# Token mixers: values stationary, two heads in the column halves, division ahead of the turn

## The reference

```python
p = jax.nn.softmax(sc, axis=-1).astype(v.dtype)          # branches a and c
return jnp.einsum('bhqk,bhkd->bhqd', p, v)
...
w = jnp.where(mask, jnp.exp(jax.nn.log_sigmoid(z) + suffix), 0.0)   # branch b
return jnp.einsum('bhqk,bhkd->bhqd', w, v)
...
g = jax.nn.sigmoid(gates.reshape(bsz, s_len, N_BRANCH, D_MODEL) + b_gate)
ys = jnp.stack([y_a, y_b, y_c], axis=2)
merged = jnp.einsum('bsnk,nkd,bsnd->bsd', ys, w_branch, g)
```

## Time and profile before

| | us |
|---|---|
| median of three runs | 2231.26 |
| the profiled execution | 2227.12 |
| its span, first to last instruction | 2225.3 |
| TensorE busy | 2011.0 (90%) |
| VectorE busy | 1413.3 (64%) |
| ScalarE busy | 850.5 (38%) |

### The profile page before, as it was taken

The page is one execution under the profiler, slowest core; times in us unless marked ns, Lnnn a source line. Parts: engine busy times, 40 slices in busy tenths (PEclk is TensorE's granted clock), DMA queues, the critical chain, the costliest instruction groups (busy, mean ns, idle before and its releaser), DMA issues.

```text
span 2225.3 us, 26662 instructions
## 1 busy us (share of the span) xinstructions
PE 2011.0 (90%) x9732; PEld 1486.1 (67%) x9732; DVE 1413.3 (64%) x2159; ACT 850.5 (38%) x1106; POOL 65.3 (3%) x93
## 2 busy tenths in 40 slices
PE   3999899989999999999988999886899879879987
PEld 2788788867887788778876887665544347654442
DVE  6888777656898888776756898775421147642111
ACT  3334555645434444555555343542200035320000
POOL 0000000000000000000000000110000001000000
PEclk9999999999999999999999999997899989989999
DMA  9898444426897799554425898541799985359997
GB/s 397 353 368 348 180 180 142 143 94 245 332 375 303 279 368 375 197 180 137 154 107 192 321 376 296 186 148 51 282 422 421 421 323 206 96 187 410 421 421 310
DMA packets 98178, 597.91 MB, mean 269 GB/s; under 512 B 20240, under 2 KB 23696, under 8 KB 27408
## 3 DMA queue, kind: packets, MB, share of 16 engines
q1 hardware_dynamic: 91600, 585.18, 67.1%
q10 hardware_dynamic: 6464, 11.15, 1.6%
HBM read 595.21 MB, written 1.09 MB: 268 GB/s over the span
## 4 chain that ended last, share of the span: by engine, by line
PE 64%; DVE 12%; DMA 12%; ACT 5%; issue 4%; POOL 1%; SPq 0%; ACTq 0%; DVEq 0%; POOLq 0%
PE acc L1950 10%; PE acc L1953 9%; PE acc L1954 9%; PE gu L2299 9%; PE gu L1950 6%; PE gu L1954 5%; PE gu L1953 5%; PE tr L2299 5%; DMA w_raw<-wstream 4%; DMA proj<-ada_stream 4%; DVE w_lo L1159 3%; PE tr L2048 3%; PE acc L2299 3%; DMA stage<-wstream 2%; ACT w_hi L654 2%
## 5 line engine op out<-in xcount | busy, mean ns | idle before, releaser
L1159 DVE TENSOR_TENSOR w_lo<-stage,w_hi 128x2048 fp32r<-128x2048 f32 x233 | 532.1, 2287 | 76.9 <-ACT w_hi L654 76.5
L654 ACT ACTIVATE w_hi<-stage 128x2048 fp32r<-128x2048 f32 x233 | 444.5, 1912 | 247.6 <-PE acc L1954 243.6
L1217 DVE SCALAR_TENSOR_TENSOR proj<-proj,c_row 128x1024 f32<-128x1024 f32 x240 | 291.6, 1218 | 52.9 <-DMA proj<-ada_stream 41.9
L1950 PE MATMUL acc<-w_hi,hT_hi 128*128 128x512 f32 (+1 forms) x736 | 307.5, 418 | 18.1 <-DVE hT_lo L1819 12.6
L1950 PE MATMUL gu<-w_hi,hT_hi 128*128 128x512 f32 x704 | 284.7, 404 | 21.3 <-DVE pair L1287 10.5
L1953 PE MATMUL acc<-w_lo,hT_hi 128*128 128x512 f32 (+1 forms) x736 | 292.1, 397 | 0.0
L1954 PE MATMUL acc<-w_hi,hT_lo 128*128 128x512 f32 (+1 forms) x736 | 291.7, 396 | 0.0
L1954 PE MATMUL gu<-w_hi,hT_lo 128*128 128x512 f32 x704 | 278.6, 396 | 0.0
L1953 PE MATMUL gu<-w_lo,hT_hi 128*128 128x512 f32 x704 | 278.2, 395 | 0.0
L1950 PE MATMUL acc<-w_hi,yT_hi 128*128 128x512 f32 (+1 forms) x460 | 183.0, 398 | 8.4 <-DVE yT_lo L1693 5.7
L1953 PE MATMUL acc<-w_lo,yT_hi 128*128 128x512 f32 (+1 forms) x460 | 180.4, 392 | 0.0
(11 more groups left out here) (224 smaller groups left out, 2333.6 us busy)
## 6 DMA issues: line engine op xcount, KB each, us to landing
stage<-wstream SPq DMA_DIRECT2D x332, 1024.0 KB, 6.0
proj<-ada_stream SPq DMA_DIRECT2D x120, 1024.0 KB, 7.8
w_raw<-wstream SPq DMA_DIRECT2D x96, 1024.0 KB, 16.8
tok<-gate_rows SPq DMA_DIRECT2D x10, 512.0 KB, 4.4
tf<-bgate_in ACTq DMA_DIRECT2D x12, 256.0 KB, 4.7
proj<-rel_in ACTq DMA_DIRECT2D x16, 192.0 KB, 2.4
z_mix<-wstream SPq DMA_DIRECT2D x2, 1024.0 KB, 17.4
once<-wstream SPq DMA_DIRECT2D x2, 1024.0 KB, 24.9
```

The source lines that it names most:

```text
L654: act.activation(w_hi[:, n % PARTS, :], stage[:, n % STAGES, :], ACT.Copy).then_inc(hi_ready, 1)
L1159: dve.tensor_tensor(w_lo[:, n % PARTS, :], stage[:, n % STAGES, :], w_hi[:, n % PARTS, :].bitcast(F32), ALU.subtract).then_inc(chunk_ready, 1)
L1217: ins = dve.scalar_tensor_tensor(w, w, 1.0, c_row[:], ALU.mult, ALU.mult, accum_out=dst)
L1950: ins = pe.matmul(dst, l_hi, r_hi, start=start, stop=False, skip_group_check=True)
```

## The change

- **out_pair** takes the place of out, once for two heads in even slots (2, 4, ... 22) and at the end, ahead of the weights' turn or suffix. The values (128 keys x 64) are stationary, the turned weights move (256 columns for the first key tile, 128 for the second); head e of the pair writes rows 64 e to 64 e + 63 of one bank, so the result is the output turned. Pairs 0 to 7 use acc, pairs 8 to 11 tr.
- **divide** on VectorE scales prob by 1 / rsum before TensorE turns it, which waits for it (w_ready). emit becomes one copy of 128 x 256 for a pair.
- **The yT turns** are gone; y_high and y_low read the stored outputs in SBUF (mixed, split), in slots 10, 17, 21 and at the end. TensorE's B fills wait for y_ready.
- **Slots 16 to 23**: suffix waits for argument(s - 2) instead of emit; weigh waits for the last pair that read its buffer.
- **The end**: hi and lo of the last fill's chunk (that of the second B chunk after slot 23) stand behind weigh and argument of slot 23; the sigmoids of branch 1's two gate blocks stand together behind them, with no table load back; y_high and y_low of the last two pairs stand before take_block half 1 of slot 23.

```diff
-      10: [("yT", 2, 0), ("yT", 2, 1)], 11: [("sT", 2)], 12: [("sT", 3)], 17: [("yT", 0, 0), ("yT", 0, 1)]}
+      11: [("sT", 2)], 12: [("sT", 3)]}
+SLOT_SPLITS = {10: [(2, 0), (2, 1)], 17: [(0, 0), (0, 1)], 21: [(1, 0)], SLOT_HEADS: [(1, 1)]}
...
+if slot > 2 * NH and slot % 2 == 0:
+    use("oT", slot // 2 - 1)
...
-    for r in range(2):
-use("yT", 1, r)
+    use("oT", SLOT_HEADS // 2 - 1)
...
-    "mixer": dict(n=MIX_CHUNKS, u=len(MIX_TR), th=8, tf=2, req=1, src=1, sc=24, mx=16, pr=24, ov=24, st=8, mg=4,
+    "mixer": dict(n=MIX_CHUNKS, u=len(MIX_TR), th=8, tf=2, req=1, src=1, sc=24, mx=16, pr=24, ov=8, st=8, mg=4,
...
+w_ready = sem("w_ready")
+y_ready = sem("y_ready")
...
+def mixed(n, r):
+    src = mv if n == 2 else proj[:, :, (1024, 2560)[n]:(1024, 2560)[n] + 512]
+    return src[:, :, 2 * r * P:2 * (r + 1) * P].rearrange("p t (a e) -> p a t e", a=2)
+def split(dst, r):
+    return dst[:, 2 * r:2 * r + 2, :].rearrange("p a (t e) -> p a t e", t=NT)
...
         def weigh(s_):
...
-            act.wait_ge(o_full, b["ov"] + s_ - 1)
+            if s_ < 2 * NH + 2:
+                act.wait_ge(o_full, b["ov"] + NH)
+            else:
+                act.wait_ge(tr_full, b["u"] + MIX_TR["oT", s_ // 2 - 1] + 1)
...
         def y_high(n, r):
-            u = b["u"] + MIX_TR["yT", n, r]
-            act.wait_ge(tr_full, u + 1)
-            d = yT_hi[:, 2 * r:2 * r + 2, :].rearrange("p a s -> p (a s)")
-            act.activation(d, tr[:, u % 2, :], ACT.Copy).then_inc(th_ready, 1)
+            if n == 1:
+                act.wait_ge(tr_free, b["u"] + MIX_TR["oT", 2 * NH // 2 + 2 * r + 1] + 1 + 2)
+                used(MIX_PRE + MIX_FILL.index(("B", 0, 1)))
+            else:
+                act.wait_ge(o_free, b["ov"] + (4 if n == 2 else 8))
+                used(MIX_PRE + MIX_FILL.index(("B", 2, 1)) if n == 0 else 5)
+            act.activation(split(yT_hi, r), mixed(n, r), ACT.Copy).then_inc(th_ready, 1)
...
         def sigmoid(blk):
...
-            act.preload_act_table_set("natural_log_exp_and_others")
+            if n != 1:
+                act.preload_act_table_set("natural_log_exp_and_others")
...
         for s_ in range(SLOT_HEADS):
...
-            hi(n0 + c + 2)
+            if s_ < SLOT_HEADS - 1:
+                hi(n0 + c + 2)
...
-            for what in SLOT_TURNS.get(s_, []):
-                if what[0] == "yT":
-                    y_high(*what[1:])
+            for what in SLOT_SPLITS.get(s_, []):
+                y_high(*what)
...
                 weigh(s_)
-            if s_ and MIX_FILL[s_ - 1][0] == "G" and block_ends(s_ - 1):
+            if 0 < s_ < SLOT_HEADS - 2 and MIX_FILL[s_ - 1][0] == "G" and block_ends(s_ - 1):
...
+        for what in SLOT_SPLITS[SLOT_HEADS]:
+            y_high(*what)
+        hi(n0 + MIX_PRE + SLOT_HEADS + 1)
+        sigmoid(FILL_BLOCK[SLOT_HEADS - 3])
...
-        y_high(1, 0)
-        y_high(1, 1)
...
-        inv_at = {}
...
-        def emit(s_):
-            h, a = s_ % NH, s_ % 2
-            dve.wait_ge(o_full, b["ov"] + s_ + 1)
-            if s_ >= 2 * NH:
-                o = acc[:, a, 0:P].rearrange("p (q e) -> p q e", q=NT)
-                dve.tensor_copy(proj[:, :, 2560 + h * HD:2560 + (h + 1) * HD], o).then_inc(o_free, 1)
-                return
-            dve.wait_ge(dve_up, inv_at[s_])
-            for q in range(NT):
-                dst = mv[:, q, h * HD:(h + 1) * HD] if s_ < NH else proj[:, q, 1024 + h * HD:1024 + (h + 1) * HD]
-                ins = dve.tensor_scalar(dst, acc[:, a, q * P:q * P + HD], rinv[:, a, q:q + 1], None, ALU.mult)
-            ins.then_inc(o_free, 1)
+        def emit(d):
+            n = BRANCHES[d // 4]
+            if d < NH:
+                dve.wait_ge(o_full, b["ov"] + d + 1)
+                o, freed = acc[:, d % 2, 0:S], o_free
+            else:
+                u = b["u"] + MIX_TR["oT", d]
+                dve.wait_ge(tr_full, u + 1)
+                o, freed = tr[:, u % 2, 0:S], tr_free
+            at = P * (d % 4) + (0, 1024, 2560)[d // 4]
+            dst = (mv if n == 2 else proj)[:, :, at:at + P]
+            dve.tensor_copy(dst, o.rearrange("p (t e) -> p t e", t=NT)).then_inc(freed, 1)
...
         def turn_weights(s_):
-            nonlocal ups
...
-            if s_ >= 2:
-                dve.wait_ge(o_free, b["ov"] + s_ - 1)
...
-            ups += 1
-            inv_at[s_] = ups
-            dve.reciprocal(rinv[:, s_ % 2, :], rsum[:, s_ % 2, :]).then_inc(dve_up, 1)
+        def divide(s_):
+            a = s_ % 2
+            dve.wait_ge(p_ready, b["pr"] + s_ + 1)
+            own(dve.reciprocal(rinv[:, a, :], rsum[:, a, :]))
+            for q, (at, end) in enumerate(((0, 128), (128, 384))):
+                ins = dve.tensor_scalar(prob[:, a, at:end], prob[:, a, at:end], rinv[:, a, q:q + 1], None, ALU.mult)
+            ins.then_inc(w_ready, 1)
...
         def y_low(n, r):
-            u, i = b["u"] + MIX_TR["yT", n, r], 2 + 2 * BRANCHES.index(n) + r
+            i = 2 + 2 * BRANCHES.index(n) + r
...
-            dve.tensor_tensor(flat(yT_lo[:, 2 * r:2 * r + 2, :]), tr[:, u % 2, :],
-                              flat(yT_hi[:, 2 * r:2 * r + 2, :]).bitcast(F32), ALU.subtract).then_inc(tr_free, 1)
+            dve.tensor_tensor(split(yT_lo, r), mixed(n, r), split(yT_hi, r).bitcast(F32),
+                              ALU.subtract).then_inc(y_ready, 1)
...
         enter(0)
         for s_ in range(SLOT_HEADS):
...
-            if s_ >= 2:
-                emit(s_ - 2)
             if s_ + 1 < SLOT_HEADS:
...
-            lo(n0 + MIX_PRE + s_ + 2)
+            if s_ == 0:
+                divide(0)
+            if s_ < SLOT_HEADS - 1:
+                lo(n0 + MIX_PRE + s_ + 2)
...
                 argument(s_)
...
                 take_block(s_, 0)
+            for what in SLOT_SPLITS.get(s_, []):
+                y_low(*what)
...
-                if what[0] == "yT":
-                    y_low(*what[1:])
-                else:
-                    at = 2 * what[1] + (8 if what[0] == "sT" else 0)
-                    copy_turn(what, flat(qk[:, at:at + 2, :]))
+                at = 2 * what[1] + (8 if what[0] == "sT" else 0)
+                copy_turn(what, flat(qk[:, at:at + 2, :]))
+            if s_ and s_ % 2 == 0:
+                emit(s_ // 2 - 1)
...
+            if s_ + 1 < 2 * NH:
+                divide(s_ + 1)
...
                 argument(s_)
+            if s_ == SLOT_HEADS - 1:
+                emit(s_ // 2)
+                for what in SLOT_SPLITS[SLOT_HEADS]:
+                    y_low(*what)
...
                 take_block(s_, 1)
-        emit(SLOT_HEADS - 2)
-        emit(SLOT_HEADS - 1)
-        y_low(1, 0)
-        y_low(1, 1)
+        lo(n0 + MIX_PRE + SLOT_HEADS + 1)
...
                 take_block(s_, t)
...
         def turn_weights(s_):
-            pe.wait_ge(p_ready, b["pr"] + s_ + 1)
+            pe.wait_ge(w_ready, 2 * NH * l + s_ + 1)
...
         def suffix(s_):
...
-            pe.wait_ge(o_free, o0 + s_ - 1)
+            if a < 2:
+                pe.wait_ge(o_free, o0 + NH - 1 + a)
+            else:
+                pe.wait_ge(arg_ready, b["st"] + a - 1)
...
-        def out(s_):
-            h, pT = s_ % NH, probT[:, s_ % 2, :]
-            if s_ < 2 * NH:
-                copied("turn", s_)
+        def out_pair(d):
+            if d < NH:
+                copied("turn", 2 * d + 1)
+                o, full = acc[:, d % 2, 0:S], o_full
+                if d >= 2:
+                    pe.wait_ge(o_free, o0 + d - 1)
...
-                pe.wait_ge(p_ready, b["pr"] + s_ + 1)
-            if s_ >= 2:
-                pe.wait_ge(o_free, o0 + s_ - 1)
-            pitch = P if s_ < 2 * NH else HD
-            o = acc[:, s_ % 2, :]
-            def v(kt):
-                if s_ < NH:
-                    return mv[:, kt, h * HD:(h + 1) * HD]
-                at = (1024 if s_ < 2 * NH else 2560) + h * HD
-                return proj[:, kt, at:at + HD]
-            if s_ == NH:
-                pe.wait_ge(fill_out[1], f0 + 2)
-            elif s_ == 2 * NH:
-                pe.wait_ge(fill_out[1], f0 + 5)
-            small_mm(o[:, 0:HD], pT[:, 0:128], v(0))
-            small_mm(o[:, pitch:pitch + HD], pT[:, 128:256], v(0), True, False)
-            small_mm(o[:, pitch:pitch + HD], pT[:, 256:384], v(1), False, True).then_inc(o_full, 1)
+                pe.wait_ge(p_ready, b["pr"] + 2 * d + 2)
+                u = u_of("oT", d)
+                pe.wait_ge(tr_free, u + 1)
+                o, full = tr[:, u % 2, 0:S], tr_full
+            if d % 4 == 0 and d:
+                pe.wait_ge(fill_out[1], f0 + (2 if d < NH else 5))
+            for kt in range(NT):
+                for e in range(2):
+                    at = (0, 1024, 2560)[d // 4] + HD * (2 * (d % 4) + e)
+                    v = (mv if d < NH // 2 else proj)[:, kt, at:at + HD]
+                    pT = probT[:, e, 0:S] if kt == 0 else probT[:, e, S:S + P]
```

(23 more changed lines are left out.)

## The result

The changed kernel takes 2194.18 us in the median of four runs (2187.84 to 2198.06), the kernel before 2230.98 (2227.66 to 2234.28): a ratio of 0.9837, 95% interval 0.9819 to 0.9855. The prediction was 2199, with a range from 2191 to 2214. The profiled execution of the changed kernel took 2198.06 us, 29.1 less than the profiled one of before.

What follows compares the result with a forecast made beforehand. TensorE was taken to bound the slots, three waits the mixers' end. Terms gave 15.0 us in the first mixer and 17.4 in the second, together 32.4, taking the median from 2231.3 to 2199 us; range 2191 to 2214.

Steps and rivals of the forecast that it cites:

- 12 pairs of heads: Per mixer: out_pair replaces two separate products per pair at 0.94 us, gaining 0.31 us a pair, 3.7 us in all.
- slot 0: First slot of each mixer: TensorE's weight transposes wait for divide, costing 0.85 us; bounds 0 to 1.5.
- turns of the outputs: Slots 10 and 17: transposes of the branch outputs go, saving 2.10 and 0.87 us, 2.97 per mixer.
- slot 20: TensorE stalls 1.65 us ahead of its first fill where it stalled 0.3: 1.35 us lost, bounds 0.4 and 2.5.
- stalls that went: Slot 20 and ahead of the last suffix: waits of suffix for emit go, gaining 1.26 us with restarts.
- end, less its pair: Last suffix to last branch's first fill: 15.48 us becomes 7.4; gain 8.1, or 7.7 without the pair already counted.
- clock: Around the mixers' ends: half clock goes with the idle time, regaining 1.6 us in the first mixer, 4.0 in the second.
- the charge for the old products: Per pair of heads: two old products counted as 1.25 us, 1.34 less what the one beside the scores shares.
- The tiling mode: Each pair, two mode changes: priced at 0.15 us each from the experts' matmuls; at 0.39 each the pair loses 0.17.
- The cover of about 4 us: From slot 1 on: divide is queued about 4 us before TensorE wants it, so it is free there.
- the chain: Slots 18 and 19: fill, splits, product, weigh, sigmoid with table loads, next splits and product; about 16.5 us against TensorE's 14.8.
- both covers: At the end: weigh finishes under a 2.8 us fill; last emit, y_high and y_low, about 2.05 us, under the other.

## Why the prediction was right

**The sum and its place.** The sum said 15.0 and 17.4 us for the two mixers; 15.97 and 18.09 came. All of it lies where the sum put it, and the time is 4.8 us below the forecast's: 1.7 of it from the mixers, the other 3.1 is less than what two medians of this kernel differ by for equal code (those of the kernel before beside the runs here went from 2226.84 to 2231.85). The stage lost 6.1 us ahead of the last suffix, 8.1 and 9.6 from there to the branch fill, and 1.8 and 2.4 behind it. The terms, one by one, per mixer, from start to start of TensorE's instructions in the first:

| term | predicted us | measured us | by |
|---|---|---|---|
| 12 pairs of heads | 3.7 | 4.2 | slots 7 and 8 14.92 to 14.53, slots 2 and 3 14.77 to 14.35, slots 17 and 18 15.99 less the turns' 0.87 to 14.81 |
| slot 0 | -0.85 | -0.78 | fill to turn, 3.05 to 3.83 |
| turns of the outputs | 2.97 | 3.0 | slots 9 and 10: 16.62 to 14.09, less the pair; slot 17: 0.87 |
| slot 20 | -1.35 | -1.38 | 24 fill matmuls 7.36 for 5.64, less the 0.33 of before |
| stalls that went | 1.26 | 1.4 | ahead of the suffix of slot 20 and of the last one, against the same instructions in the slots beside them |
| end, less its pair | 7.7 | 7.8 | 15.48 to 7.41 |
| clock | 1.6 and 4.0 | 1.8 and 4.0 | behind the end 14.31 and 14.92 to 12.54; second end 17.05 for 15.48 |

The measured terms add up to 16.0 and 18.2, within 0.2 us of what the stages lost. The terms of turns and stalls are read from the two traces; no experiment takes them out one by one.

**The pair** was the mis-sized term. Its own cost was right (0.94 predicted, 0.95 measured), but what it replaced was worth more: it gains 0.39 to 0.41 us up to slot 15 instead of 0.31. The step that was off is the charge for the old products, 1.25 us for two; 0.95 and 0.39 make it 1.34. The lone product was taken for 0.67 us and is worth 0.72: 0.58 to the next start, and 0.14 because without it 24 fill matmuls follow each other directly and take 5.57 us, where the two fills around it took 2.85 and 2.86. The product beside the scores was taken for 0.58 and is worth 0.62. In slots 16 to 22, where a suffix and not a turn stands behind the pair, it gains only 0.3: the way back costs 0.11 us there instead of 0.06, which is half of the difference.

**The tiling mode.** The eight passes lie between matmuls of full width. Of their 0.95 us the passes themselves are 0.64, as forecast: putting the second head in the same half adds just that (1.45 for 0.80). What is left for going in and coming back is 0.31, half of it inside the 0.80, where 0.15 and 0.15 were taken from the row of the experts' stage. The Trainium skill (TensorEngine Tiling (Array Packing), Key Properties) says that a change of the tiling mode drains TensorE. The trace has a cost of some 0.15 us at each change, which agrees with it and doesn't show a drain by itself; at this price it decided nothing.

**The division** was covered in every slot but the first, and slot 0 was 0.07 us off. The cover of about 4 us, on which this stood, is there from slot 3 on (3.7 to 5.6 us from the scalings' end to the turn); in slot 1 it is 0.68 and in slot 2 2.49. Doubling the scalings still cost nothing in the other slots, but slot 1 is close: it is the one that waits when slot 0 no longer does. VectorE's share rose to 80% and no slot was set by it.

**Slots 18 to 20** went as the chain said: one stall, ended by a block product, 1.71 us for 1.65 with its restart, and it went with the sigmoid out of the chain, which gave 1.68.

**The end** came to the hundredth (7.4 predicted, 7.41 measured), since all its terms were TensorE's own durations once both covers held. Both did: weigh was 1.5 us early, the split 0.97.

**The clock.** I had counted the loss as regained because idle time of 2 to 3 us stood ahead of each fall. In the mixers' ends the half clock appears in the kernel before and with the old order put back, in all four stages that were traced, and it is absent with the new order, with and without the pair, in all twenty. This goes with the idle time, not with the values or the turns. That the idle time is the cause is not shown beyond this; the longest wait in a new end is 1.57 us. What it isn't is a fixed saving: the profiled execution of the change has a short dip behind its second mixer (0.63 from 1146 to 1151), where code is equal in all kernels here and TensorE waits 1.71 us for a low part; behind its first mixer, with the same wait, there is none.

**Where my reasons fell short** is in two expectations. The loops of out_pair were to cost 13 us in the wrong order, and cost nothing: issue order isn't what sets two halves side by side. And the old end was to cost some 7 us and the clock, and cost 12: I had not seen that the old order's chain through ScalarE keeps its length, so that what TensorE saves ahead of it comes back as a wait. In the forecast this is silent, because the new order has both weights in time, yet there it is the reason why the two parts are worth 34.1 us together and only 25.3 apart.

## What to carry to other kernels

Cost a bundle of edits together at the place where they meet: here what the direct output saves at the end came back as a wait for late inputs, and only the reordering that brought these forward let it pay. Where a small product runs beside large ones, price also the restart that each interruption gives the work behind it. When an engine gets extra work, look for the one slot where its cover isn't yet there, the first, and for the one where it sits in a chain with no slack; both are cheap to mend by moving the work one slot.

## What was unexpected of the hardware

Two heads in the two column halves overlap whatever the order of issue: with four passes of one issued ahead of the other's the eight took 0.81 us, interleaved 0.80, and in one half 1.45. For the rest, the chip did what the trace of before had led me to expect.
